# Attention values computed as transposed pairs of heads, with the probabilities normalised before they are transposed

## The chip, the cores and the metric

The kernel runs on one core of a Trainium2 chip. The metric is device microseconds of one execution. The kernel before was timed in three runs: the median is 1093.15 us, from 1092.9 to 1095.22 us.

## The reference

A model of three layers works on one sequence of S = 256 tokens with 1024 channels, in float32. Layer 0 mixes eight "fox" heads and eight "dsa" heads of width 64 (dsa: each query keeps only its 64 best keys, chosen by an index score). Layer 1 has sixteen "moba" heads of width 64; at this length they are causal. Both are followed by a gated feed-forward part with a short convolution. Layer 2 ("second block") mixes eight latent-attention heads ("mla", width 64, mask by chunks of 64) and four mLSTM heads ("ml", width 128), and is followed by a mixture of 32 experts and a gated per-layer embedding. All 36 softmax or mLSTM heads end in the same way, here for softmax:

```python
s = where(mask, (q @ k.T) * scale, -1e30)      # 256 queries x 256 keys, per head
pr = softmax(s, axis=-1)
out[:, h*64:(h+1)*64] = pr @ v                 # per head
x = x + concatenate(all heads) @ w_out         # 1024 x 1024
```

## The kernel before

The program is written by hand for each engine: `tensor` (TensorE, PE), `vector` (VectorE, DVE), `scalar` (ScalarE, ACT), `gpsimd` (POOL) and `sync` (the DMA queue). Every engine executes its own list strictly in order, and semaphores join them. `claim` and `take` give out one of the eight PSUM banks and wait until its last user was drained; `filled` and `emptied` wait for a bank to be complete or drained. Weights (1 MB units) stream into a ring of seven slots (twelve in the expert stage). Each weight chunk is split into a high part (`wh`, ACT, `split_hi`) and a low part (`wl`, DVE, `split_lo`), three chunks deep; activations are split likewise (`hh`/`hl`, `mh`/`ml`), and a product is the three terms high x high, high x low and low x high in the fast float32r format. `out_steps` (L667) computes the output projection of a layer in 16 steps: eight slices k of 128 input channels, each for two tiles t of 128 queries, six matmuls of 512 columns per step.

The attention part of each layer is a software pipeline written out by hand, of 21 iterations i in layers 0 and 1 and of 15 in layer 2. In iteration i PE computes the scores of head h = i (`score_T`, L710), transposes the probabilities of head i-2 (`probs_T`, L700: three 128 x 128 transposes, since query tile 0 sees only key tile 0) and computes the values of head i-3 (`value_T`, L717). Between these it runs steps of the projections of the same layer (`proj`, or `z_pieces` in layer 2), of `side` work (the dsa index and mask in layer 0) and of `out_steps`. Iterations 8 and 9 have no new head in layers 0 and 1: there the second group of eight heads is prepared (in layer 0, POOL rotates the dsa queries, L2625, and PE transposes them into `dqT`). DVE adds the mask and takes row maxima (`maxima`, L1948), ACT takes the exponential and row sums (`probs`, L1363), and the transposed probabilities are copied to `ptb` by ACT or, for even heads of layer 1, by DVE (`evac_P`).

In `value_T` the transposed probabilities (128 keys x 128 queries) are the stationary operand and the 64 value columns of the head move: three matmuls per head, which all write 64 columns of two banks, one for each query tile. After the eighth head of a group DVE divides both banks by the row sums into `mix` (`finish`, L1958), PE transposes `mix` (`mixT`, L840: eight transposes per group, in iteration 10 or 11 for the first group and after the loop for the second; once in layer 2), and ACT and DVE split the result into `mh` and `ml` (`mix_hi` L1372, `mix_lo` L1967). Only then can the slices of that group enter `out_steps`.

In layer 2 the mLSTM heads have a longer way: DVE's `hm_steps` (L2374) normalise the outputs of the four heads (its last step signals `s_hm`), PE transposes them (`hmT`), and DVE and ACT apply the gate and split them; slices k = 4 to 7 of the output projection wait for that. `z_pieces` (L1088) are eight pieces of a projection, handed out in the iterations `z_steps` (L505).

## Time and profile before

| | |
|---|---|
| median of 3 runs | 1093.15 us |
| the profiled execution | 1093.0 us |
| its span, first to last instruction | 1090.9 us |
| PE busy | 1040.6 us (95%) |
| DVE busy, ACT busy | 621.6 us (57%), 521.4 us (48%) |
| granted TensorE clock, mean | 0.983 of 2.4 GHz |
| chain that ended last | PE 89%, DVE 6%, ACT 2% |

The numbers of a stretch or a line come from views of the trace: the timeline lists instructions in order of time, adjacent ones of one kind merged, with the start, the busy time and, in brackets, how long the engine stood idle before it and what released it. A float32 matmul leaves two records (each passes over its columns), a float32r matmul or a transpose one. Records overlap, so the price of a group is the distance from its start to the start of what follows. A form such as 128*64 128x512 means a stationary operand of 128 rows and 64 columns and a moving one of 128 rows and 512 columns.

### The profile page before, as it was taken

What the parts mean: (1) busy time and instruction counts of PE and PEld (TensorE: products, weight loads), DVE (VectorE), ACT (ScalarE), POOL (GpSimd) and SP (SyncE); (2) the same over time, 40 slices, a digit from 0 to 9 for tenths busy, and PEclk for the clock granted to TensorE, in tenths of its full rate; (3) what the DMA queues carried; (4) which work ended last, traced back from release to release, by engine and by line L of the source; (5) the groups of instructions that cost most, each with busy time, mean ns of one, the idle gap of its engine ahead of it and who ended that gap; (6) DMA issues with size and microseconds to landing.
All of it is one profiled execution on the core that took longest, in us unless ns stands there. A gap on an engine that the chain in (4) does not pass through costs nothing.

```text
span 1090.9 us, 15541 instructions
## 1 busy us (share of the span) xinstructions
PE 1040.6 (95%) x6143; PEld 816.4 (75%) x6143; DVE 621.6 (57%) x1167; ACT 521.4 (48%) x902; POOL 90.2 (8%) x104
## 2 busy tenths in 40 slices
PE   6998999999999999899999999989899999999977
PEld 5777789999888877799999888778754545445435
DVE  4677467888746556468888647646662221122146
ACT  5755555555535454456556435755442212122145
POOL 0101001121100311001212101100000000000000
PEclk9999899999999999999999999998989999999999
DMA  8824136655554633245565564207629999999931
GB/s 282 292 78 154 40 116 186 201 157 195 190 192 155 220 117 105 74 145 190 170 201 170 194 180 137 94 30 244 234 75 393 409 408 407 409 409 409 406 127 39
DMA packets 112672, 224.63 MB, mean 206 GB/s; under 512 B 10559, under 2 KB 65234, under 8 KB 112594
## 3 DMA queue, kind: packets, MB, share of 16 engines
q1 hardware_dynamic: 112434, 223.04, 58.1%
q8 instruction: 51, 0.84, 0.3%
q10 hardware_dynamic: 160, 0.53, 0.1%
q14 instruction: 27, 0.22, 0.1%
HBM read 222.50 MB, written 1.05 MB: 205 GB/s over the span
## 4 chain that ended last, share of the span: by engine, by line
PE 89%; DVE 6%; ACT 2%; DMA 1%; issue 1%; POOL 0%; SPq 0%; DVEq 0%; POOLq 0%; ACTq 0%
PE ps L527 84%; PE ps L531 5%; DVE wl L1825 1%; DMA ring<-in_w_uv_dram 1%; ACT hh L1310 1%; DMA cst<-in_const_dram 0%; DVE hl L1835 0%; DVE ml L1825 0%; ACT wh L1313 0%; DVE xs L1825 0%; DVE smb L1839 0%; POOL sA L2625 0%; DVE sA L1835 0%; ACT L1310 0%; ACT sA L1310 0%
## 5 line engine op out<-in xcount | busy, mean ns | idle before, releaser
L1825 DVE TENSOR_TENSOR wl<-ring,wh 128x1024 fp32r<-128x1024 f32 (+3 forms) x212 | 278.2, 1322 | 124.9 <-ACT wh L1313 123.3
L1313 ACT ACTIVATE wh<-ring 128x1024 fp32r<-128x1024 f32 (+3 forms) x212 | 222.5, 1053 | 150.3 <-PE ps L527 148.2
L527 PE MATMUL ps<-hh,wh 128*128 128x256 f32 x768 | 219.5, 287 | 1.3 <-DVE big L1830 1.2
L527 PE MATMUL ps<-hh,wl 128*128 128x256 f32 x768 | 217.2, 284 | 0.0
L527 PE MATMUL ps<-hl,wh 128*128 128x256 f32 x768 | 215.5, 284 | 0.0
L527 PEld LDWEIGHTS ps<-hh,wh 128*128 128x128 f32 x768 | 147.9, 193 | 2.4 <-DVE big L1830 1.5
L527 PEld LDWEIGHTS ps<-hh,wl 128*128 128x128 f32 x768 | 147.9, 193 | 0.0
L527 PEld LDWEIGHTS ps<-hl,wh 128*128 128x128 f32 x768 | 146.9, 193 | 0.3
L527 PE MATMUL ps<-ring,xg 128*64 128x512 f32 x320 | 85.5, 595 | 0.0
L527 PE MATMUL ps<-wh,hh 128*128 128x512 f32 (+3 forms) x192 | 80.1, 417 | 5.3 <-DVE wl L1825 5.1
L2654 POOL TENSOR_TENSOR fs<-fs,rt 128x256 f32<-128x256 f32 x44 | 52.5, 1212 | 324.3 <-ACT fs L1310 324.3
L527 PE MATMUL ps<-wl,hh 128*128 128x512 f32 (+3 forms) x192 | 75.2, 391 | 0.0
L527 PE MATMUL ps<-wh,hl 128*128 128x512 f32 (+3 forms) x192 | 73.6, 391 | 0.0
L1835 DVE SCALAR_TENSOR_TENSOR ysl<-ps,wsl,ysh 128x512 fp32r<-128x512 f32 x32 | 24.0, 751 | 83.0 <-ACT ysh L1310 83.0
L1835 DVE SCALAR_TENSOR_TENSOR fa<-ps,rsl,fs 128x256 f32<-128x256 f32 x16 | 7.7, 484 | 105.7 <-ACT fs L1310 105.7
L527 PEld LDWEIGHTS ps<-ring,xg 128*64 128x64 f32 x320 | 26.4, 137 | 50.4 <-issue 50.3
L527 PE MATMUL ps<-ringx,xg 128*64 128x512 f32 x192 | 57.6, 592 | 0.0
L1310 ACT ACTIVATE fs<-ps,rsl 128x256 f32<-128x256 f32 x16 | 7.6, 476 | 101.4 <-PE ps L527 101.4
L527 PE MATMUL ps<-wl,ffh 128*128 128x512 f32 x176 | 54.9, 389 | 0.0
L527 PE MATMUL ps<-wh,ffl 128*128 128x512 f32 x176 | 54.9, 389 | 0.0
L527 PE MATMUL ps<-wh,ffh 128*128 128x512 f32 x176 | 54.8, 389 | 0.0
L1839 DVE CUSTOM_DVE_ANT_0 smb<-ps,cst 128x128 f32<-128x128 f32 x72 | 25.7, 357 | 44.3 <-PE ps L527 42.7
(273 smaller groups left out, 1719.9 us busy)
## 6 DMA issues: line engine op xcount, KB each, us to landing
ring<-in_w_up_dram SPq DMA_DIRECT2D x88, 512.0 KB, 4.9
ring<-in_w_down_dram SPq DMA_DIRECT2D x22, 1024.0 KB, 4.9
ring<-in_w_gate_e_dram SPq DMA_DIRECT2D x40, 512.0 KB, 7.9
ring<-in_w_up_e_dram SPq DMA_DIRECT2D x40, 512.0 KB, 11.1
ringx<-in_w_down_e_dram SPq DMA_DIRECT2D x16, 1024.0 KB, 10.1
ring<-in_w_down_e_dram SPq DMA_DIRECT2D x16, 1024.0 KB, 11.3
ring<-in_w_in_odd_dram SPq DMA_DIRECT2D x12, 1024.0 KB, 5.0
ringx<-in_w_gate_e_dram SPq DMA_DIRECT2D x24, 512.0 KB, 9.8
```

What stands on the lines that cost most here:

```text
L527: return e.matmul(o, l, r, start=start, stop=stop)
L531: return e.transpose(o, i, cst[0:n, C_ID:C_ID + n])
L1310: return e.activation(o, i, f, **kw)
L1313: return e.activation(o, i, ACT.Copy)
L1825: return e.tensor_tensor(o, a, b, op)
L1835: return e.scalar_tensor_tensor(out=o, in0=a, scalar=s, in1=b, op0=o1, op1=o2)
L1839: return e.tensor_tensor_reduce(out=o, in0=a, in1=b, scale=1.0, scalar=init, op0=o1, op1=o2, accum_out=ac)
L2654: e.tensor_tensor(fs[:, f % 2, :], fs[:, f % 2, :], rb, ALU.mult).then_inc(s_silr, 1)
```

## The change

`value_pair` takes the place of `value_T` for all heads of width 64 (the mLSTM heads keep `value_T`). The values of a head (128 keys x 64 columns) are now the stationary operand and the transposed probabilities move: one matmul of 256 queries for key tile 0 and one of 128 queries for key tile 1. The result is already transposed (64 channels x 256 queries). An even head writes partitions 0 to 63 of the bank and the odd head after it partitions 64 to 127, so that a bank holds four heads, which are two slices k of the output projection. The pair is computed in the iteration of its odd head.

Since queries now lie along the free axis, the division by the row sums moves ahead of the transposes. DVE inverts the sums of each head (`inverted`), and the probabilities are multiplied in place, in two instructions: by ACT for the fox heads and the even moba heads, by DVE for the dsa, the odd moba and the mla heads (`normed`). `probs_T` waits for `s_pn` in place of `s_p`. `finish`, `mixT` and the copy by which DVE made one of the high parts are gone; ACT makes all of them (`mix_hi`) and DVE subtracts (`mix_lo`), one bank at a time, in iterations 8, 10 and 17 and after the loop (layer 0), 11 or 12, 17 and after (layer 1), 10 and after (layer 2).

The output projection runs as one generator over all eight slices: ten, eight and four steps of it are handed out in or right after the loops of layers 0, 1 and 2 (before: seven, seven, none). The z pieces of layer 2 end in iteration 11 and not after the loop, and the mLSTM normalisation has one more of its steps inside the loop. The first four slices of layer 2 have split buffers of their own, and one ring slot of the expert stage is loaded only after slice 3.

```diff
-        out_at = ((12, 13, 14, 15, 16, 18, 19), (13, 14, 15, 16, 17, 18, 19))
-        z_steps = (0, 2, 4, 6, 8, 10, 12, 14)
+        out_at = (range(11, 21), range(13, 21), range(12, 15))
+        z_steps = (0, 2, 4, 6, 8, 9, 10, 11)
...
                 if g in SP:
-                    q.wait_ge(s_p, SP[g])
+                    q.wait_ge(s_pn, SP[g])
...
+            def value_pair(name, bt, vals, ptb):
+
+                def f(h):
+                    n, j = h // 4, h // 2 % 2
+                    gs = [G[name][h - 1], G[name][h]]
+                    b = claim(bt[n], name, n) if j == 0 else bank[bt[n]]
+                    for t in range(2):
+                        for a, g in enumerate(gs):
+                            w = mm(b[64 * a:64 * a + 64, j * S + t * P:(j + 1) * S], vals(h - 1 + a, t),
+                                   ptb[:, g % 3, 2 * t * P:(t + 2) * P], t == 0, t == 1)
...
-            value = [value_T("fox", 8, 64, lambda h, t: big1[:, t, 1024 + h * 64:1088 + h * 64], (0, 1), ptb1),
-                     value_T("dsa", 8, 64, lambda h, t: dv[:, t, h * 64:h * 64 + 64], (6, 7), ptb1)]
-
-            def mixT(layer, g, src):
...
+            value = [value_pair("fox", (0, 1), lambda h, t: big1[:, t, 1024 + h * 64:1088 + h * 64], ptb1),
+                     value_pair("dsa", (6, 7), lambda h, t: dv[:, t, h * 64:h * 64 + 64], ptb1)]
...
-            rotation[:] = [4, 5, 6, 7]
-            mixT(2, 0, "mla")
-            for _ in out_steps((2, "out"), c_outm, range(0, 3), 8, mh3, ml3, mixed(2), high=mixed_high(2)):
-                pass
+            next(outp)
+            rotation[:] = [4, 5, 7, 0]
             q.wait_ge(s_hm, 1)
...
+            def normed(g, h, pb, count):
+
+                q.wait_ge(s_rs, count)
+                act(pb[:, g % 3, 0:P], pb[:, g % 3, 0:P], ACT.Copy, scale=rsi[:, 0, h:h + 1])
+                act(pb[:, g % 3, P:384], pb[:, g % 3, P:384], ACT.Copy, scale=rsi[:, 1, h:h + 1]).then_inc(s_pn, 1)
...
+            def inverted(g, h):
+
+                q.wait_ge(s_p, SP[g])
+                return rcp(rsi[:, :, h:h + 1], rs[:, :, h:h + 1])
+
+            def normed(g, h, pb):
+
+                own.inc(inverted(g, h))
+                for c, t in ((slice(0, P), 0), (slice(P, 384), 1)):
+                    w = ts(pb[:, g % 3, c], pb[:, g % 3, c], rsi[:, t, h:h + 1], None, ALU.mult)
+                    if t == 0:
+                        own.inc(w)
+                w.then_inc(s_pn, 1)
+
+            def mix_lo(name, n, hi_, lo_, count):
+
+                b = filled(q, name, n)
+                q.wait_ge(s_mhi, count)
+                tt(lo_, b[:, :], hi_.bitcast(F32), ALU.subtract).then_inc(of(drained, name, n), 1)
...
+                h = head_at.get(i - 1)
+                if h is not None:
+                    if h < 8:
+                        inverted(h, h).then_inc(s_rs, 1)
+                    else:
+                        normed(h, h, pb1)
+                if i in (8, 10, 17):
+                    n = (8, 10, 17).index(i)
+                    filled(q, ("even", 4), 1)
+                    mix_lo(("fox", "dsa")[n // 2], n % 2, bank_of(mh1, n), bank_of(ml1, n), n + 1)
...
+                if i >= 1 and i <= 12 and order2[i - 1][0] == "mla":
+                    normed(32 + i - 1, order2[i - 1][1], pb3)
...
-                if 10 <= i < 13:
+                if 10 <= i < 14:
                     next(hms)
-            q.wait_ge(s_xn, 2)
-            finish("mla", 8, lambda t: mix[:, t, 0:512])
-            gate_rows(3)
-            mix_lo(2, 0, mh3, ml3, 5)
             for _ in hms:
                 pass
-            for k in range(3):
-                split_lo(c_outm + k + 3, wh, wl)
+            mix_lo("mla", 1, mla_hi[:, 1, :], mla_lo[:, 1, :], 10)
+            split_lo(c_outm + 5, wh, wl)
...
+                elif k == NU + 4:
+                    q.wait_ge(s_mlo, 2)
+                    q.wait_ge(*chunk_done[c_outm + 3])
```

## Rows read from the trace of the kernel before

**Rows 1.** The page, part 1: busy time by engine, over the whole span.
```profile
PE 1040.6 (95%) x6143; PEld 816.4 (75%) x6143; DVE 621.6 (57%) x1167; ACT 521.4 (48%) x902; POOL 90.2 (8%) x104
```

**Rows 2.** PE timeline, layer 0: start, busy us, engine, line, operation; one head's values.
```profile
84.14 0.78 PE L527 MATMUL ps<-big,ptb 128*128 128x64 f32 x6
84.75 1.08 PE L527 MATMUL ps<-ring,sA 128*128 128x512 f32 x2
```

**Rows 3.** PE timeline: one float32 matmul on the whole array; then experts, alternating column halves.
```profile
79.51 1.02 PE L527 MATMUL ps<-ring,sA 128*128 128x512 f32 x2
80.36 0.82 PE L527 MATMUL ps<-mb,big 66*128 66x128 f32 x4
...
854.51 3.60 PE L527 MATMUL ps<-ring,xg 128*64 128x512 f32 x16
857.95 3.60 PE L527 MATMUL ps<-ringx,xg 128*64 128x512 f32 x16
861.48 0.50 PE L527 MATMUL ps<-S__12,xh 128*128 128x256 f32 x2
```

**Rows 4.** PE timeline, layer 2: matmuls in one column half only.
```profile
695.55 3.67 PE L527 MATMUL ps<-big,ring 128*64 128x256 f32 x16
699.15 1.98 PE L527 MATMUL ps<-ring,big 128*128 128x512 f32 x4
```

**Rows 5.** PE timeline, layer 0, between the fox and the dsa heads.
```profile
105.14 1.97 PE L531 MATMUL ps<-cst,big 128*128 128x128 f32 x8 [1.49 <-POOL big L2625]
...
109.43 1.97 PE L531 MATMUL ps<-cst,xs 128*128 128x128 f32 x8
...
114.97 0.88 PE L531 MATMUL ps<-cst,pb 128*128 128x128 f32 x3 [1.98 <-DVE mxb L1839]
```

**Rows 6.** PE timeline, layer 0, after its loop.
```profile
140.01 1.25 PE L531 MATMUL ps<-cst,xs 128*128 128x128 f32 x8 [1.14 <-DVE xs L1825]
141.02 0.71 PE L527 MATMUL ps<-wh,mh 128*128 128x512 f32 x2
```

**Rows 7.** PE timeline, layer 1: the seam between its groups, and after its loop.
```profile
438.08 0.52 PE L531 MATMUL ps<-cst,pb 128*128 128x128 f32 x3 [1.80 <-DVE ptb L1843]
...
461.87 0.33 PE L531 MATMUL ps<-cst,xs 128*128 128x128 f32 x1 [1.07 <-DVE xs L1825]
```

**Rows 8.** PE timeline, layer 2, from the last values to the next norm.
```profile
752.76 1.54 PE L527 MATMUL ps<-big,ptb 128*128 128x64 f32 x6 [1.92 <-ACT ptb L1313]
...
756.77 1.91 PE L531 MATMUL ps<-cst,xs 128*128 128x128 f32 x8
...
767.33 0.72 PE L527 MATMUL ps<-wh,mh 128*128 128x512 f32 x2 [2.38 <-DVE wl L1825]
...
785.34 1.91 PE L531 MATMUL ps<-cst,x 128*128 128x128 f32 x16
```

**Rows 9.** DVE timeline: a reciprocal, a scaling of 256 columns, and the mLSTM's last step.
```profile
98.98 0.35 DVE L1830 TENSOR_SCALAR top<-top,st 128x256 f32<-128x256 f32 x1
...
102.68 0.25 DVE L1851 RECIPROCAL rsi<-rs 128x16 f32<-128x16 f32 x1
...
764.92 1.22 DVE L1825 TENSOR_TENSOR xs<-xs,st 128x1024 f32<-128x1024 f32 x1
```

**Rows 10.** DVE timeline, dsa heads: from one head's maxima over a weight split to the next.
```profile
125.77 0.29 DVE L1839 CUSTOM_DVE_ANT_0 smb<-ps,sA 128x128 f32<-128x128 f32 x1 [2.37 <-PE ps L527]
...
126.65 1.22 DVE L1825 TENSOR_TENSOR wl<-ring,wh 128x1024 fp32r<-128x1024 f32 x1
129.10 0.29 DVE L1839 CUSTOM_DVE_ANT_0 smb<-ps,sA 128x128 f32<-128x128 f32 x1 [1.24 <-PE ps L527]
```

**Rows 11.** ACT timeline: a scaling of 256 columns.
```profile
716.90 0.38 ACT L1310 ACTIVATE mb<-ps 128x256 f32<-128x256 f32 x1
```

**Rows 12.** Windows: length, busy us by engine, PE clock, DMA share, GB/s.
```profile
745.00:760.00 15.00, 12.77 (x80) 12.01 (x79) 9.87 (x22) 7.94 (x19) 0.00 (x0) 0.77 0.58 181
...
940.00:980.00 40.00, 40.00 (x210) 19.76 (x210) 9.48 (x17) 9.30 (x21) 0.00 (x0) 1.00 1.03 409
```

More of the change, by code:

```diff
@@ L450, in build, with halves, tiles, bank_of @@
         hsq = smb3[:, :, :].rearrange("p a b -> p (a b)")[:, 0:1024].rearrange("p (t h d) -> p t h d", t=2, d=P)
+        def halves(v):
+            return [v[:, j * S:(j + 1) * S] for j in range(2)]
+        def tiles(v, ks):
+            return [v[:, k, :] for k in ks]
+        def bank_of(v, n):
+            return v[:, 2 * n:2 * n + 2, :].rearrange("p k s -> p (k s)")
         def aT(c, g):
@@ L907, in tensor @@
                     rotation[:] = [4, 5]
-                if i == 10:
-                    rotation[:] = [0, 1]
-                    mixT(0, 0, "fox")
-                    rotation[:] = [4, 5]
-                    outp = out_steps((0, "out"), c_oute, range(4), 8, mh1, ml1, mixed(0), high=mixed_high(0))
             rotation[:] = [4, 5, 6, 7]
-            mixT(0, 1, "dsa")
             for _ in outp:
-                pass
-            for _ in out_steps((0, "out"), c_oute, range(4, 8), 8, mh1, ml1, mixed(0), high=mixed_high(0)):
                 pass
@@ L1483, in scalar @@
             next(proj)
-            outp = iter(())
+            outp = ahead(c_oute, 8)
             for i in range(21):
+                h = head_at.get(i - 1)
+                if h is not None and h < 8:
+                    normed(h, h, pb1, h + 1)
                 h = head_at.get(i - 2)
@@ L1507, in scalar @@
                         evac(flat(dqT[:, 2 * j:2 * j + 2, :]), "dqT", j)
-                if i == 10:
-                    mix_hi(0, 0, mh1)
-                    outp = ahead(c_oute, 4)
-            next(outp)
-            mix_hi(0, 1, mh1)
+                if i in (8, 10, 17):
+                    n = (8, 10, 17).index(i)
+                    mix_hi(("fox", "dsa")[n // 2], n % 2, bank_of(mh1, n))
+            mix_hi("dsa", 1, bank_of(mh1, 3))
             for _ in outp:
                 pass
-            for k in range(4, 8):
-                split_hi(c_oute + k + 3, wh)
             def ffn(l):
@@ L1571, in scalar @@
             next(proj)
-            outp = iter(())
+            outp = ahead(c_outo, 8)
             for i in range(21):
+                h = head_at.get(i - 1)
+                if h is not None and h % 2 == 0:
+                    normed(16 + h, h, pb2, 9 + h // 2)
                 h = head_at.get(i - 2)
@@ L2157, in vector @@
                     next(side, None)
-                if i == 10:
-                    filled(q, ("even", 4), 1)
-                    mix_lo(0, 0, mh1, ml1, 1)
-                    outp = ahead(c_oute, 4)
-            filled(q, "dsa", 1)
-            finish("dsa", 8, lambda t: mix[:, t, 512:1024], 8)
-            next(outp)
-            mix_lo(0, 1, mh1, ml1, 2)
+            mix_lo("dsa", 1, bank_of(mh1, 3), bank_of(ml1, 3), 4)
             for _ in outp:
                 pass
-            for k in range(4, 7):
-                split_lo(c_oute + k + 3, wh, wl)
             add_x((0, "out"))
@@ L2255, in vector @@
                     moba_T(1, i - 8)
-            finish("moba1", 8, lambda t: mix[:, t, 512:1024], 8)
-            next(outp)
-            mix_lo(1, 1, mh2, ml2, 4)
+            mix_lo("moba1", 1, bank_of(mh2, 3), bank_of(ml2, 3), 8)
             for _ in outp:
                 pass
-            for k in range(4, 7):
-                split_lo(c_outo + k + 3, wh, wl)
             add_x((1, "out"))
```

215 lines of the change are left out of this document (108 added, 107 removed).

## The prediction

> **What bounds the kernel now.** I read the page first: PE is busy 1040.6 us of a 1090.9 us span [rows 1], so only 50 us are idle, and a change pays if it takes time off PE's own list or fills its idle stretches. Next the view of PE's waits, which places the idle time, and the timelines of PE, DVE and ACT around the three attention loops. There the waits sit at the seams of the head groups: for POOL's rotation and for DVE's maxima in layer 0 [rows 5], for DVE's copy in layer 1 and DVE's division after the loops [rows 6, 7], for ACT's copy and DVE's weight split in layer 2 [rows 8]. Inside the loops PE has no gaps. The expert stage behind them has none either, but its DMA share is 1.03 at 409 GB/s [rows 12], which is a rival below.
>
> **Part 1, the value matmuls.** Before, one head costs 84.75 - 84.14 = 0.61 us in six records [rows 2], a pair 1.22 us. After, each head has two records of 256 columns and two of 128. A float32 record of 512 columns takes (80.36 - 79.51)/2 = 0.43 us on the whole array; in the expert stage 16 such records that alternate between the column halves take 3.44 us, 0.215 us each [rows 3]. So the halves run at the same time. In one half alone a 256-column record takes 3.60/16 = 0.225 us [rows 4], so its weight load is hidden. A pair is then 2 x 0.225 + 2 x 0.11 = 0.67 us; the run that is followed by whole-array work lasts 3.53 instead of 3.44 us [rows 3], 0.09 us for a switch, taken twice: 0.87 us, a saving of 0.35 us. Bounds: without the overlap 2 x 0.67 + 0.2 = 1.54 us (a loss of 0.32); with no switch cost and perfect overlap 0.64 us (a gain of 0.58). I take 0.87, because the expert rows have the same alternation, type and stationary width. There are 4 fox, 4 dsa, 8 moba and 4 mla pairs.
>
> The Trainium skill speaks against this: TensorE: Matmul & The Clock Gate, section Part 3: Packing small matmuls, says that weight loads overlap running matmuls only if the row group differs, and two column halves share their rows. By that rule the eight loads of a pair would be exposed. The trace does not agree, at least at 512 columns: 0.215 us leaves no room for a load [rows 3].
>
> **Part 2, transposes and division removed.** Eight transposes cost 141.02 - 140.01 = 1.01 us at full clock [rows 6] and up to 1.97 us at the low one [rows 5]; there are five groups. With them go the waits for DVE's division, 1.14 and 1.07 us [rows 6, 7]. What is late next behind the loops: the last bank needs ACT's high part and DVE's low part, about 1.3 us. The generator still has slices of earlier banks to run (k = 5 in layer 0, k = 4 and 5 in layer 1), at least 2.7 us, so nothing of it shows.
>
> **Part 3, work added.** A DVE-normalised head costs a reciprocal (0.25 us) and two scalings (0.35 us, and at most that for 128 columns) [rows 9], 0.9 us with the gaps; an ACT-normalised one about 0.25 + 0.38 [rows 11], 0.65 us, and 0.25 us on DVE. That is 24 heads on DVE (8 dsa, 8 odd moba, 8 mla) and 16 on ACT (8 fox, 8 even moba). In the dsa and second moba loops DVE needs 0.88 us for the maxima, 1.2 us for a split every second iteration and now 0.9 us, 2.4 us in all, against 3.33 us per iteration [rows 10], of which PE saves 0.2. It fits, at no cost. The new wait of `probs_T` comes an iteration after the normalisation, so it normally finds it done.
>
> **Part 4, seam of layer 0.** In iterations 3 to 7 DVE is already nearly full with the mask; five reciprocals and ACT's scalings ahead of `even_evac(4)` delay POOL's rotation. PE's saving on the fox pairs is lost in that wait, and I add 0.75 us: `dqT` transposes at 105.9 and not 105.14 [rows 5]. In return `mixT` (1.97 us) goes and only one `mix_lo` (0.7 us, after its high part) stands between the maxima of heads 8 and 9. The first output step claims bank 1, which that `mix_lo` drains, so PE still waits, but by 118.9 us two output steps are done where one was done at 118.15. One step is 1.4 us. Net gain 0.65 us. Dsa pairs: 4 x 0.35 = 1.4. Behind the loop 1.14 + 1.01 = 2.15. **Layer 0: 4.2 us.**
>
> **Part 5, layer 1.** Moba pairs: 8 x 0.35 = 2.8, with PE full around them. At the seam the 1.80 us wait [rows 7] is for DVE's copy behind `mix_lo`; with `normed` (0.9) and two subtractions (1.3) in place of three instructions (2.0) that copy comes as late as before, and the vanished `mixT` is swallowed by the wait: 0.2. Behind the loop 1.07 + 1.0. **Layer 1: 5.1 us.**
>
> **Part 6, layer 2.** Before, PE ends at 785.34, after waits of 1.92 and 2.38 us, a `mixT` of 1.91 and cold z pieces [rows 8], with a mean clock of 0.77 [rows 12]. I moved the lists of PE, DVE and ACT forward. PE gets to the end of iteration 11 at 750.0 (before, iteration 12 began at 747.3; two z pieces of some 1.6 us each now stand ahead of it, less what the pairs save). There a new wait appears: `normed` of the last head stands behind 2.5 us of mLSTM work on DVE, PE waits about 1.3 us in iteration 13 (and 2.5 if the weight split of iteration 11 counts fully). Four output steps are done by 759.2. DVE's last mLSTM step ends at 761.0 instead of 764.92 + 1.22 = 766.1 [rows 9]. Then `hmT` 0.9, slices 2 and 3 (5.4), a wait of 0.4 for slice 4's split, slices 4 to 7 (10.9): 778.6, a gain of 6.7. PE still idles twice there and the clock will be low in part as before; I take off 1.5. **Layer 2: 5.2 us.**
>
> **Sum.** 4.2 + 5.1 + 5.2 = 14.5 us off the profiled execution of 1093.0 us, which stands at the median (1093.15): 1078.5 us.
>
> **Rivals.** (a) *The halves do not overlap, or the loads of short records are exposed.* A pair costs 1.54 us. For: the expert records are of 512 columns, these of 128 and 256. Against: the rows of part 1 [rows 3, 4]. 16 pairs count (the fox ones are covered): 16 x 0.67 = 10.7 us less gain, 1089 us. Half of it, 1084, if only the loads show.
>
> (b) *The weight stream of the experts sets the end.* The share is 1.03 [rows 12]. Then all that is gained ahead is lost: 1093 us. Against: PE has no wait there, 40.00 of 40 us, and the queue's waits are for PE to free slots, so PE sets the pace.
>
> (c) *Slower: DVE's `normed` stalls every transpose.* If DVE's list per iteration gets longer than PE's, 3.1 us, each of 24 heads puts its 0.9 us on the path: 21.6 us against a gain of 14.5, 1100 us. Its place is the second half of each loop, and it decides once DVE needs over 3.1 us; I count 2.4, so some 0.7 us of unseen waits per head are wanted.
>
> (d) *More than forecast:* the seams close, the clock stays at 2.4 GHz in layer 2 (1.5 us back), and PE gets the fox pairs (1.4), the seams of layers 0 and 1 (2 to 4): 1072 us.
>
> **Chances.** Forecast (1074 to 1083) 0.60; (a) with its half, 0.13; (b) 0.04; (c) 0.07; (d) 0.16. A measurement here can tell about 0.2%, 2.2 us, from no change. Faster: 0.60 + 0.16 + 0.12 = 0.88; same 0.05; slower 0.07. The range takes (d) and the half of (a): 1071 to 1086.
>
> **What would show it.** A pair should start its successor 0.87 us later (part 1); no transposes of `xs` but the eight of the mLSTM (part 2); no PE idle of a microsecond behind the loops of layers 0 and 1 (part 2); the `dqT` transposes of layer 0 at about 105.9 us, later than before in spite of a faster PE (part 4); the next norm of layer 2 about 14.5 us earlier, and every later stage moved by just that (part 6, and against (b)). It would be wrong if `probs_T` rows carry waits for DVE in mid-loop, or if pairs cost over 1.2 us.

## The result and the profile after

The changed kernel takes 1088.24 us (median of 9 runs, 1085.35 to 1090.53); the kernel before, timed beside it, 1095.22 us (median of 9, 1092.62 to 1101.16). The ratio is 0.9919, with a 95% interval from 0.9899 to 0.9939: some 7 to 9 us faster, where 14.5 were forecast. The direction was right, the size about half, and the time lies 2 us above the upper end of the range. (Timed once more below, the change gave 10.4 us by the medians.)

The profiled execution of the changed kernel took 1089.69 us with a span of 1087.9 us. That is only 3.0 us less than the span before, because the profiled execution of the kernel before is among its fastest (1093.0 us) and this one is slower than its median: the two profiles show where time went, and the medians how much. Page, part 1 (answers to [rows 1]):

```profile
PE 1034.5 (95%) x6023; PEld 795.9 (73%) x6023; DVE 628.7 (58%) x1235; ACT 533.7 (49%) x939; POOL 89.7 (8%) x104
```

PE has 120 records less, DVE and ACT have 68 and 37 more. The mean granted clock was 0.976 of 2.4 GHz, in the execution before 0.983. A first account: span times the missing share of the clock is 1090.9 x 0.017 = 18.5 us before and 1087.9 x 0.024 = 26.1 us after (an upper bound of what the clock cost, since a low clock costs nothing while PE idles). What is left is 1072.4 against 1061.8 us. So by this estimate 10.6 us were gained by work and waits, and up to 7.6 us went to the clock, between these two executions. Not between the kernels as a whole: over the executions timed in the groups below, the median clock of the kernel before was 0.977 or 0.978, that of the changed kernel's 15 executions 0.976. The stages say where the two profiles differ. Each cell is the distance between two starts on PE: from the transposes of the last fox head to the transposes of the next norm (layer 0), and from one norm's transposes to the next (layers 1 and 2, experts).

| us | layer 0, from the seam | layer 1 | layer 2 | experts |
|---|---|---|---|---|
| before | 153.40 - 101.64 = 51.76 | 475.24 - 342.49 = 132.75 | 785.34 - 664.23 = 121.11 | 1057.90 - 785.34 = 272.56 |
| after | 153.06 - 102.47 = 50.59 | 470.72 - 342.14 = 128.58 | 780.55 - 659.72 = 120.83 | 1053.82 - 780.55 = 273.27 |

Layer 1 gave 4.2 us, layer 0 counted from the start only 0.34 (its last fox head came 0.83 us later), layer 2 only 0.28. The experts took 0.7 us more and what follows them 1.1 us more (34.1 against 33.0; 32.9 in the second profile of the changed kernel), which makes up the 3.0 us.

**Layer 0.** PE timeline of the changed kernel from the last fox head on (columns as in [rows 2], to be held against [rows 5]):

```profile
102.47 0.55 PE L546 MATMUL ps<-cst,pb 128*128 128x128 f32 x3 [2.07 <-ACT pb L1326]
103.80 1.05 PE L542 MATMUL ps<-ptb,big 128*64 128x256 f32 x8 [0.78 <-ACT ptb L1329]
104.78 1.97 PE L546 MATMUL ps<-cst,big 128*128 128x128 f32 x8
107.52 1.66 PE L542 MATMUL ps<-sA 64*128 64x128 f32 x8 [0.78 <-ACT sA L1329]
109.11 0.79 PE L542 MATMUL ps<-wh,mh 128*128 128x512 f32 x1
112.61 0.79 PE L542 MATMUL ps<-wh,mh 128*128 128x512 f32 x1 [2.70 <-DVE ml L1853]
...
120.00 1.65 PE L542 MATMUL ps<-sA 64*128 64x128 f32 x4
```

The wait for POOL in [rows 5] is gone, and the query transposes start at 104.78, before 105.14. But the first output step issues one matmul and then stands for 2.70 us at the bank that the second fox evacuation has to drain. DVE and ACT at that moment, from their timelines:

```profile
109.29 0.29 DVE L1867 CUSTOM_DVE_ANT_0 smb<-ps,sA 128x128 f32<-128x128 f32 x1 [4.62 <-PE ps L542]
...
111.86 0.69 DVE L1853 TENSOR_TENSOR ml<-ps,mh 128x512 fp32r<-128x512 f32 x1 [1.60 <-ACT mh L1329]
```

```profile
110.29 0.40 ACT L1326 ACTIVATE pb<-smb,nbb 128x128 f32<-128x128 f32 x1 [2.91 <-DVE nbb L1858]
...
111.19 0.57 ACT L1329 ACTIVATE mh<-ps 128x512 fp32r<-128x512 f32 x1
```

The bank was complete at about 104.8, where the row of its last pair ends. Both engines then idled, DVE for 4.62 us and ACT for 2.91, and turned to the next head's maxima and exponentials first, because those stand ahead of the evacuation in their lists. After this stall the records stay long: windows of 6 us (columns as in [rows 12]) of the kernel after, then before:

```profile
109.00:115.00 6.00, 3.30 (x8) 1.78 (x6) 3.11 (x14) 3.00 (x10) 0.00 (x0) 0.50 0.01 3
115.00:121.00 6.00, 6.00 (x17) 4.20 (x17) 2.74 (x9) 1.76 (x6) 0.00 (x0) 0.50 0.00 0
121.00:127.00 6.00, 6.00 (x22) 3.96 (x21) 2.61 (x15) 2.90 (x8) 0.00 (x0) 0.68 0.00 0
```

```profile
109.00:115.00 6.00, 4.02 (x19) 2.57 (x17) 3.66 (x14) 1.47 (x5) 0.00 (x0) 0.50 0.00 0
115.00:121.00 6.00, 6.00 (x25) 4.57 (x26) 2.66 (x12) 4.57 (x15) 0.00 (x0) 0.76 0.01 3
```

PE is busy for all of 115 to 121 in both, but does 17 records in one and 25 in the other: the clock is at its lower level, 1.2 GHz, to about 124 us instead of 118.

**Layer 1.** PE timeline, then DVE timeline:

```profile
435.36 0.81 PE L546 MATMUL ps<-cst,pb 128*128 128x128 f32 x3 [1.81 <-DVE ptb L1871]
...
455.63 0.55 PE L546 MATMUL ps<-cst,pb 128*128 128x128 f32 x3 [1.53 <-DVE pb L1858]
```

```profile
454.10 0.69 DVE L1853 TENSOR_TENSOR ml<-ps,mh 128x512 fp32r<-128x512 f32 x1 [3.62 <-ACT mh L1329]
```

The first wait is the one of [rows 7], as forecast. The second is new: DVE stood 3.62 us in front of `mix_lo` of iteration 17, for ACT's high part, and the last head's division was queued behind it. The waits behind the loop are gone.

**Layer 2.** PE, DVE and ACT timelines (to be held against [rows 8]):

```profile
718.18 1.08 PE L542 MATMUL ps<-big 2*128 2x128 f32 x4 [1.59 <-DVE rs L1867]
...
750.17 0.90 PE L546 MATMUL ps<-cst,pb 128*128 128x128 f32 x3 [3.29 <-DVE pb L1858]
...
763.24 1.09 PE L546 MATMUL ps<-cst,xs 128*128 128x128 f32 x8 [1.89 <-DVE xs L1853]
```

```profile
746.75 0.69 DVE L1853 TENSOR_TENSOR mla_lo<-ps,mla_hi 128x512 fp32r<-128x512 f32 x1 [3.15 <-ACT mla_hi L1329]
...
748.37 0.29 DVE L1867 CUSTOM_DVE_ANT_0 smb<-ps,cst 128x128 f32<-128x128 f32 x1
...
749.44 0.68 DVE L1858 TENSOR_SCALAR pb<-pb,rsi 128x128 f32<-128x128 f32 x2
```

```profile
745.09 1.05 ACT L1329 ACTIVATE wh<-ring 128x1024 fp32r<-128x1024 f32 x1
746.03 0.58 ACT L1329 ACTIVATE mla_hi<-ps 128x512 fp32r<-128x512 f32 x1
```

The same pattern: `mix_lo` of iteration 10 held DVE for 3.15 us, since ACT makes the high part at the end of its own iteration 10, behind a weight split. The maxima of the last head (head 11 of the 12), whose scores PE had long computed, came only at 748.37, and behind them, at 749.44, the division of head 10. It is head 10 whose transposes PE waits for at 750.17, in iteration 12. In the windows (after, then before) there is also a new stretch at the low clock early in the loop, behind the wait at 718.18:

```profile
715.00:727.00 12.00, 10.41 (x54) 9.05 (x52) 6.65 (x30) 4.14 (x13) 0.00 (x0) 0.72 0.01 2
```

```profile
715.00:727.00 12.00, 11.21 (x73) 9.69 (x72) 5.98 (x28) 6.68 (x20) 0.00 (x0) 0.99 0.00 0
```

### The profile page after: what moved, and what is told of

It reads as the page before. It is cut to its first block, busy times and chain, and to the rows that moved or that the text cites. A ratio compares the mean times of both kernels' runs of the same rounds, so it can differ in the third digit from the quotient of the medians.

```text
span 1087.9 us, 15372 instructions
## 1 busy us (share of the span) xinstructions
PE 1034.5 (95%) x6023; PEld 795.9 (73%) x6023; DVE 628.7 (58%) x1235; ACT 533.7 (49%) x939; POOL 89.7 (8%) x104
## 4 chain that ended last, share of the span: by engine, by line
PE 86%; DVE 7%; ACT 4%; DMA 1%; issue 1%; SPq 0%; DVEq 0%; ACTq 0%
PE ps L542 81%; PE ps L546 4%; DVE wl L1853 1%; ACT pb L1326 1%; DMA ring<-in_w_uv_dram 1%; DVE smb L1867 1%; ACT hh L1326 1%; ACT wh L1329 0%; DMA cst<-in_const_dram 0%; DVE hl L1863 0%; DVE xs L1853 0%; DVE smb L1853 0%; ACT xh L1329 0%; ACT L1326 0%; ACT xg L1326 0%
## 5 line engine op out<-in xcount | busy, mean ns | idle before, releaser
L1326 ACT ACTIVATE ysh<-ps,wsl 128x512 fp32r<-128x512 f32 x32 | 22.0, 687 | 58.9 <-PE ps L542 58.9
```

What stands on the lines that cost most here:

```text
L1326: return e.activation(o, i, f, **kw)
```

## The experiments

**The theory** (W, later Q, for queue): the change's own savings are there, and half of them is lost to DVE and ACT evacuations that stand in the wrong place of two in-order lists, and to the low clock that follows the stalls. Its rivals: the clock's chance in one execution (C), the work on column halves keeping the clock low (V), DVE's or ACT's work itself as the bound (D, A), and the division as the whole cause.

The runs were timed in three groups, each on another chip with the kernel before beside it. Its median was 1098.26 us in the first group (the changed kernel once more, the early fox bank, the mLSTM steps, both heads in one half), 1097.88 in the second (the first latent bank, no division, the four moves, all eight latent heads on ACT) and 1095.87 in the third (steps one iteration later, the four moves again, six latent heads on ACT). The changed kernel was in the first group only. For the other two, a difference from it is therefore given by way of the kernel before: the lead over the kernel before beside it, less the 10.4 us that the changed kernel had.

### The changed kernel once more

> The changed kernel once more, unchanged, as the yardstick of the runs beside it. Theory W (the new waits are a property of the order of work): the same idle stretches as in its first profile stand at the same places, 2.70 us at 112.61 behind the evacuation of the fox bank, 1.59 us at 718.18, 3.29 us at 750.17, and the stretches at the lower TensorE clock follow them (to about 124 us in layer 0). Rival C (the small gain is the clock's chance of one execution): the waits stay, but the low stretch of layer 0 ends near 118 us as in the kernel before, layer 0 ends 2 us or more earlier than 153.1, and the time comes out near 1083.

Measured: 1087.9 us (median of 6, 1085.51 to 1091.14), ratio to before 0.9899 (0.9858 to 0.9941), 10.4 us by the medians. The waits stand where they stood: 2.70 us for `ml`, 1.58 for `rs`, 3.29 and 1.51 for `pb`, and layer 0 takes 51.36 us from the seam, with the clock low to about 125. C falls for layer 0. One wait is new, 0.98 us for the last head's division in iteration 13 of layer 2.

### The second fox bank evacuated early

First ACT in iteration 9, then DVE at the head of iteration 10:

```diff
+                    mix_hi("fox", 1, bank_of(mh1, 1))
                     for j in range(2):
                         evac(flat(dqT[:, 2 * j:2 * j + 2, :]), "dqT", j)
-                if i in (8, 10, 17):
+                if i in (8, 17):
...
+                    filled(q, ("even", 4), 1)
+                    mix_lo("fox", 1, bank_of(mh1, 1), bank_of(ml1, 1), 2)
                     for _ in side:
                         pass
```

> The changed kernel with one thing moved: the evacuation of the second fox bank (ACT's high part, DVE's low part) goes ahead of the dsa queries' evacuation on ACT and to the head of iteration 10 on DVE, where both engines idle (2.3 and 4.6 us), instead of behind the eighth head's maxima and exponentials. Theory W: the 2.70 us wait of the first output step on bank 1 is gone, TensorE is busy through 109 to 113 us, its clock rises near 118 us as before instead of 124, and layer 0 ends about 3.5 us earlier (149.5 instead of 153.1): time 3 to 4.5 us below the changed kernel. Rival V (work on column halves keeps the clock low): the wait goes, but the low stretch still ends at 122 us or later, and the gain is under 2 us.

Measured: 1083.86 us (1079.82 to 1085.24), 4.0 us below, ratio 0.9859 (0.9817 to 0.9900); the two intervals overlap, but the slowest of these runs is faster than the fastest of the changed kernel beside it. The wait is gone. Windows:

```profile
109.00:115.00 6.00, 4.61 (x26) 2.97 (x26) 3.31 (x17) 3.55 (x11) 0.00 (x0) 0.94 0.01 3
115.00:121.00 6.00, 6.00 (x31) 4.17 (x30) 4.61 (x20) 4.50 (x13) 0.00 (x0) 1.00 0.00 0
```

31 records in 115 to 121 instead of 17. From the seam layer 0 took 147.32 - 105.06 = 42.26 us, 8.3 less than in the first profile of the changed kernel. Four later profiles with the early bank give 42.18 to 42.77 us; four with the changed kernel's own layer 0, the first among them, 48.63 to 51.36. The profile gives twice what the median does: this execution reached its seam 2.6 us later, and its layer 1 took 1.5 us more than the same code did before. The time is as expected, the clock is not: it was full from about 110.6, before the first output step, and not from 118. V falls: the pairs on column halves are the same here and the clock is full.

### The output steps begun one iteration later

```diff
-        out_at = (range(11, 21), range(13, 21), range(12, 15))
+        out_at = (range(12, 21), range(13, 21), range(12, 15))
```

> The changed kernel with the output projection's steps of layer 0 begun in iteration 12 instead of 11 (on all engines), and nothing else moved: the wait on the second fox bank, which the first step claims, must vanish by name, but no work takes its place in iteration 11. Theory F (what the early evacuation gained was work for TensorE in the seam, and through it the clock): TensorE idles through most of 109 to 113 all the same, now behind ACT's and DVE's work on the first dsa heads, the clock is low to 118 us at least, and one step more stands after the loop: within 2 us of the changed kernel. Rival N (it is the wait itself that costs): 2.5 us or more below the changed kernel, as with the early evacuation.

Measured: 1084.0 us (1082.68 to 1086.26), ratio 0.9882 (0.9847 to 0.9917), 11.9 us below the kernel before: 1.5 us more than the changed kernel's lead, and the intervals of the two ratios overlap almost whole. (The bare medians differ by 3.9 us, but the kernel before was 2.4 us faster in this group too.) I had expected under 2. PE timeline:

```profile
110.45 0.92 PE L542 MATMUL ps<-sA 64*128 64x128 f32 x4 [0.93 <-DVE mxb L1867]
114.61 0.90 PE L546 MATMUL ps<-cst,pb 128*128 128x128 f32 x3 [3.23 <-DVE pb L1858]
```

```profile
109.00:115.00 6.00, 1.84 (x12) 1.04 (x10) 3.52 (x17) 2.45 (x9) 0.00 (x0) 0.73 0.00 0
115.00:121.00 6.00, 6.00 (x23) 4.11 (x21) 2.76 (x15) 3.59 (x10) 0.00 (x0) 0.71 0.01 3
```

PE idles as I said, even more (1.84 of 6 us busy). But the stalled step had held back what stood behind it in PE's list: the scores of head 10 start at 110.45 here and at 115.04 in the changed kernel, so DVE and ACT go on meanwhile. From the seam layer 0 takes 150.64 - 102.80 = 47.84 us. By these single profiles, 2.8 of the 8.3 us that the early evacuation won from the seam come from not letting PE stand in front of that bank, and the other 5.6 need the bank drained early, so that PE has work in the seam. The clock was full at 108.60 here too (0.93 us for the eight score records, 1.66 in the changed kernel), but behind the wait of 3.23 us it was low again, to about 118. So in these profiles the clock rose at that point with either order, and stayed up only where PE had work. The time is what theory F expected; N, which wanted 2.5 us or more, is not borne out.

### The mLSTM steps moved back

```diff
-                if 10 <= i < 14:
+                if 11 <= i < 15:
                     next(hms)
```

> The changed kernel with the mLSTM epilogue's steps on DVE begun one iteration later in layer 2, so that the last head's division stands ahead of the large step instead of behind it. Theory W: the 3.29 us wait at 750.17 falls under 0.7 us, the low clock of 748 to 757 us goes for the most part (2 us), while the epilogue ends up to 2.5 us later and the wait of the epilogue's transposes (1.89 us at 763.24) grows by about as much: layer 2 ends 1 to 3 us earlier. Rival D (the chain of DVE's work sets the end of layer 2): the wait reappears whole at the epilogue's transposes, and layer 2 ends within 0.7 us of 780.55.

Measured: 1091.06 us (median of 12, 1088.55 to 1096.37), 3.2 us above the changed kernel by the medians, ratio 0.9935 (0.9907 to 0.9963), which overlaps the changed kernel's; the profiled execution, 1095.81 us, is one of the five slower ones of the twelve. Layer 2 took 784.33 - 660.05 = 124.28 us, against 120.83 and 122.08 in the two profiles of the changed kernel. PE timeline:

```profile
749.45 0.84 PE L546 MATMUL ps<-cst,pb 128*128 128x128 f32 x3 [2.27 <-DVE pb L1858]
...
764.39 1.97 PE L546 MATMUL ps<-cst,xs 128*128 128x128 f32 x8 [5.01 <-DVE xs L1853]
```

The wait at head 10 fell by 1.0 us, and the wait for the epilogue grew by 3.1. Only the small first mLSTM step (747.36 to 748.2 in the changed kernel's DVE rows) stood between `mix_lo` and this division, and delaying the steps gave no gain. So theory W, too, had the wrong holder for this wait; the DVE rows of layer 2 above name the right one, `mix_lo`. The large step, which the prediction had named, stands ahead of head 11's division and is not at issue at 750.17.

### The first latent bank evacuated one iteration later by DVE

```diff
-                if i == 10:
+                if i == 11:
                     q.wait_ge(s_xn, 2)
                     mix_lo("mla", 0, mla_hi[:, 0, :], mla_lo[:, 0, :], 9)
```

> The changed kernel with DVE's evacuation of the first latent bank moved from iteration 10 to iteration 11 of layer 2, behind that iteration's maxima and division, so that DVE no longer stands 3.15 us before it for ACT's high part (746.75 in the changed kernel's trace) with the next head's maxima queued behind. Theory Q (the 3.29 us wait of TensorE at 750.17 is DVE's queue behind that evacuation, not the mLSTM's steps as the prediction had it): the wait falls under 1 us, the low clock of 748 to 757 us goes, the epilogue's chain starts some 3 us earlier too, and layer 2 ends 3 to 5 us earlier (117 us or less from nm2's transposes to nf2's, instead of 120.8): 3 to 4.5 us below the changed kernel. Rival D (DVE's own work in iterations 10 to 14 is what TensorE waits for): most of the wait comes back one iteration later and the gain is under 1 us.

Measured: 1086.59 us (1084.21 to 1088.99), ratio 0.9889 (0.9856 to 0.9922): a lead of 11.3 us over the kernel before, about 1 us more than the changed kernel's, less than expected, and not told from it by the intervals. In the trace layer 2 took 776.54 - 661.83 = 114.71 us, 6.1 less than in the first profile (four profiles with the old order here gave 117.5 to 122.1), and its clock was 1.00 in both stretches where it had been low, 718 to 730 and 747 to 759:

```profile
747.95 0.50 PE L542 MATMUL ps<-wh,mla_hi 128*128 128x512 f32 x1 [1.29 <-DVE mla_lo L1853]
751.45 0.55 PE L546 MATMUL ps<-cst,pb 128*128 128x128 f32 x3 [1.25 <-DVE pb L1858]
759.27 1.09 PE L546 MATMUL ps<-cst,xs 128*128 128x128 f32 x8 [2.10 <-DVE xs L1853]
```

The wait of 3.29 us for head 10 is gone: the theory names the right instruction. In its place an output step waits 1.29 us for the moved `mla_lo`, and head 11 waits 1.25 us in iteration 13, the wait that the prediction had forecast (1.3 us); so the rival is right that DVE's work comes due soon after (DVE is busy 11.21 us of 12 in 747 to 759). The waits together fell by only 0.7 us; by this one profile, most of the rest is the clock.

### The division left out

```diff
-                own.inc(inverted(g, h))
-                for c, t in ((slice(0, P), 0), (slice(P, 384), 1)):
-                    w = ts(pb[:, g % 3, c], pb[:, g % 3, c], rsi[:, t, h:h + 1], None, ALU.mult)
...
-                w.then_inc(s_pn, 1)
+                inverted(g, h).then_inc(s_pn, 1)
```

(and `normed` on ACT with its calls; the reciprocal of each head now releases its transposes)

> The changed kernel without the division itself: the reciprocals stay and release the transposes, the 16 divisions on ACT (0.80 us each) and the 24 on DVE (0.67 us each) are left out, so that the probabilities go undivided into the value products. It prices what part 3 of the prediction set at nothing. If part 3 holds, the time stays within 1.5 us of the changed kernel. Theory Q expects 3 to 6 us less: 0.8 us off each of the waits on pb at 99.05, 102.47, 140.68, 455.63 and 750.17 and off the bank wait at 718.18, and what the clock gives back with them; the waits behind the mix evacuations (2.70 at 112.61, most of 3.29 at 750.17) stay. If the division were the whole cause of the missing half, it would be 8 us or more.

This kernel leaves the division by the row sums out, so its values are not the model's. Measured: 1080.36 us (median of 4, 1077.08 to 1083.99), ratio 0.9845 (0.9802 to 0.9888): a lead of 17.5 us over the kernel before, 7.1 more than the changed kernel's (5.9 by the ratios). The remaining waits of the transposes are now on the reciprocal:

```profile
101.61 0.55 PE L546 MATMUL ps<-cst,pb 128*128 128x128 f32 x3 [1.96 <-DVE rsi L1875]
...
739.41 0.55 PE L546 MATMUL ps<-cst,pb 128*128 128x128 f32 x3 [2.58 <-DVE rsi L1875]
```

Every layer is shorter, 46.34, 126.07 and 116.63 us, and the waits at 99.05, 140.68 and 455.63 are gone. So the division costs some 6 to 7 us with this order of work, at or above the upper end of what I expected, and not far from the 8 us that would have made it the whole cause. But it isn't: the next run keeps every division and gains more, 2.7 us in the same group.

### Four evacuations moved, nothing removed

Four moves in DVE's list, of six banks in all: the early fox bank (shown above, on ACT too), the first dsa and the first moba1 bank, moba0's two banks, and the first latent bank. In layer 1 the copy `evac_P` now comes ahead of the block of moba0:

```diff
-                if i in (8, 10, 17):
-                    n = (8, 10, 17).index(i)
+                if i in (8, 18):
+                    n = (8, 10, 18).index(i)
...
+                if i == 18:
+                    mix_lo("moba1", 0, bank_of(mh2, 2), bank_of(ml2, 2), 7)
+                h = head_at.get(i - 2)
+                if h is not None and h % 2 == 0:
+                    evac_P(16 + h, ptb2)
                 if i == 12:
                     filled(q, ("odd", 5), 1)
                     for n in range(2):
                         mix_lo("moba0", n, bank_of(mh2, n), bank_of(ml2, n), 5 + n)
-                if i == 17:
-                    mix_lo("moba1", 0, bank_of(mh2, 2), bank_of(ml2, 2), 7)
-                h = head_at.get(i - 2)
-                if h is not None and h % 2 == 0:
-                    evac_P(16 + h, ptb2)
...
-                if i == 10:
+                if i == 11:
                     q.wait_ge(s_xn, 2)
```

> The changed kernel with four evacuations of DVE put elsewhere in its queue, nothing added or taken away: the second fox bank early (as in the run before it), the first dsa and moba1 banks one iteration later (18 instead of 17), moba0's two behind the copy of the transposed probabilities in iteration 12, the first latent bank in iteration 11. Theory Q: the waits at 112.61 (2.70), 435.36 (1.81), 455.63 (1.53), 140.68 (0.5) and 750.17 (3.29) go or fall under 0.7, and with them most of the low clock in 434 to 440 and 748 to 757: 8 to 12 us below the changed kernel, near 1077, which is what the prediction gave for the change. Rival D: the gains don't add up since DVE's work comes due again, and it ends within 2 us of the seam's edit alone (4 us below the changed kernel).

> The kernel with the four moved evacuations once more, as the yardstick beside the next run: 10 us below the changed kernel, 18 to 21 below the kernel before.

Measured: 1077.61 us (1072.32 to 1078.30), ratio 0.9801 (0.9767 to 0.9836), and again 1074.77 us (1071.97 to 1076.97), ratio 0.9796 (0.9760 to 0.9831). That is 20.3 and 21.1 us below the kernel before beside it, with all of the change's work in it, and 9.9 and 10.7 us more than the changed kernel's lead, as expected of theory Q. The waits of PE that are left in layers 1 and 2 (timeline):

```profile
425.64 0.87 PE L546 MATMUL ps<-cst,pb 128*128 128x128 f32 x3 [0.62 <-DVE ptb L1872]
...
735.84 0.50 PE L542 MATMUL ps<-wh,mla_hi 128*128 128x512 f32 x1 [1.29 <-DVE mla_lo L1854]
739.34 0.55 PE L546 MATMUL ps<-cst,pb 128*128 128x128 f32 x3 [1.27 <-DVE pb L1859]
747.16 1.09 PE L546 MATMUL ps<-cst,xs 128*128 128x128 f32 x8 [2.10 <-DVE xs L1854]
```

and the seam of layer 0 (windows):

```profile
109.00:115.00 6.00, 6.00 (x24) 4.12 (x23) 4.92 (x22) 4.29 (x14) 0.00 (x0) 0.83 0.01 3
115.00:121.00 6.00, 6.00 (x34) 4.18 (x34) 4.59 (x18) 3.90 (x11) 0.00 (x0) 1.00 0.00 0
```

The stages take 42.18, 125.75 and 116.11 us (42.18, 125.78 and 116.16 the second time); the mean clock is 0.988 and 0.987. Over all executions its median is 0.984 and 0.986, against 0.976 in the changed kernel: by the same upper bound as above, 9 to 11 us, so the removed waits and the clock behind them can't be told apart in this gain. Nor does this run show that the moves need the change: the kernel before, whose clock is low in the seam of layer 0 too, was not reordered.

### The latent heads divided by ACT

On top of the four moves, first ACT's list of layer 2, then DVE's; a second version does so for the first six heads only:

```diff
+                if 1 <= i <= 12 and order2[i - 1][0] == "mla":
+                    normed(32 + i - 1, order2[i - 1][1], pb3, 17 + order2[i - 1][1])
...
-                    normed(32 + i - 1, order2[i - 1][1], pb3)
+                    inverted(32 + i - 1, order2[i - 1][1]).then_inc(s_rs, 1)
```

> The four moved evacuations, and in layer 2 the eight latent heads' divisions on ACT (1.60 of its 3 us busy at most in a slice) in place of DVE. Theory Q: the bank wait at 718.18 (1.59 us, DVE's reciprocal, division and weight split ahead of the evacuation) falls to about 0.8, its low clock of 718 to 727 goes (3 us), at no cost on ACT: 1 to 4 us below the run with the four moves alone. Rival A (ACT turns late instead): a wait on ACT's pb of 1 us or more stands in iterations 3 to 12, and it is no faster than the four moves alone.

> The four moved evacuations, and in layer 2 the first six latent heads' divisions on ACT, the last two on DVE, since with all eight on ACT the last one waited 2.60 us on ACT for DVE's reciprocal and held up ACT's weight split and through it DVE's epilogue chain (4.00 us wait at 748.00). Theory Q: the bank wait at 708 keeps its 0.86 us instead of 1.58, the last two heads wait as in the run with the four moves (1.3 us each), the epilogue's transposes wait 2.1 to 2.8 us, and the time is 1 to 2.5 us below the four moves alone. Rival D (the end of layer 2 is DVE's epilogue chain whatever comes ahead of it): within 1 us of the four moves alone.

Measured: 1075.46 us (1074.32 to 1077.88), ratio 0.9794 (0.9761 to 0.9826), with all eight on ACT, 2.2 us below the four moves in the same group; 1076.63 us (1073.48 to 1078.52), ratio 0.9803 (0.9766 to 0.9839), with six, 1.9 us above the four moves in its group, where theory Q wanted 1 to 2.5 below. Neither can be told from the four moves alone. The bank wait fell to 0.86 us as expected, and with all eight on ACT the price came back at the epilogue (PE, then DVE timeline):

```profile
748.00 1.97 PE L546 MATMUL ps<-cst,xs 128*128 128x128 f32 x8 [4.00 <-DVE xs L1856]
```

```profile
741.04 1.23 DVE L1856 TENSOR_TENSOR wl<-ring,wh 128x1024 fp32r<-128x1024 f32 x1 [2.47 <-ACT wh L1329]
```

DVE, freed of the divisions, waits 2.47 us for a weight split that ACT reaches late; layer 2 took 119.46 us in this profile, against 116.11 with the four moves alone. Six on ACT avoids that (2.10 us at the epilogue) and still gains nothing measurable. That fits rival D for the end of layer 2.

### Both heads of a pair in one half

```diff
-                    for t in range(2):
-                        for a, g in enumerate(gs):
-                            w = mm(b[64 * a:64 * a + 64, j * S + t * P:(j + 1) * S], vals(h - 1 + a, t),
+                    for a, g in enumerate(gs):
+                        for t in range(2):
+                            w = mm(b[0:64, j * S + t * P:(j + 1) * S], vals(h - 1 + a, t),
```

> The changed kernel with the second head of every pair written to the same partition half of the bank as the first, one head after the other (the second head's values overwrite the first's, and the upper half of the bank is not computed): same matmuls, same columns, no two of them in different halves. Part 1 of the prediction says that the halves run at once: a pair of 8 records then costs 1.3 us (768 columns at the 0.43 us per 512 of two passes each way) instead of 0.80, and 20 pairs cost up to 10 us, some of it hidden in the waits of layer 2 and of the seam: time 6 to 10 us above the changed kernel. The rival of part 1 (halves don't run at once, the loads set the pace): the pair stays at 0.8 to 0.9 us and the time moves by under 2 us.

This kernel leaves out the upper half of each bank and overwrites one head's values with the other's. Measured: 1096.55 us (median of 10, 1095.27 to 1100.68), 8.7 us above the changed kernel in the same group; ratio to before 0.9996 (0.9967 to 1.0024). The groups of fox, moba and latent values, by form, of the changed kernel and of this one (busy us in total, mean ns):

```profile
L542 PE MATMUL ps<-ptb,big 128*64 128x256 f32 x64 | 10.9, 420 | 0.8 <-ACT ptb L1329 0.8
L542 PE MATMUL ps<-ptb,big 128*64 128x128 f32 x64 | 6.7, 288 | 0.0
```

```profile
L542 PE MATMUL ps<-ptb,big 128*64 128x256 f32 x64 | 20.3, 399 | 0.8 <-ACT ptb L1329 0.8
L542 PE MATMUL ps<-ptb,big 128*64 128x128 f32 x64 | 12.6, 279 | 0.0
```

17.6 us become 32.9 for 16 pairs. A merged pair row goes from 0.87 to 1.51 us; from its start to the start of what follows, where nothing waits, a pair goes from 0.80 to 1.45 us (127.64 to 128.44 in the changed kernel, 133.04 to 134.49 here). 20 pairs at 0.65 us would be 13 us; 8.7 show in the time. With nothing but the side-by-side placement gone, the kernel is as slow as the one before.

## Why the prediction was half right

**Part 1 (the pair) held.** 0.87 us were forecast from one start to the next (its own terms, 0.67 + 2 x 0.09, add up to 0.85). Measured that way a pair costs 0.80 us, so it saves 0.42 us and not 0.35; that the merged row also reads 0.87 is chance, since such a row overlaps its successor. In one half a pair costs 1.45 us, where the prediction had 1.54 for no overlap. The bound of rival (a) is about right and the rival itself is refuted by the run in one half. The change covers 20 pairs, 40 of the kernel's 44 heads (not 36, as the section on the reference has it). The Trainium skill (TensorE: Matmul & The Clock Gate, Part 3: Packing small matmuls) says that weight loads overlap running matmuls only if the row group differs. This case's rows don't agree, for records of 128 and 256 columns either: the eight loads of the pair at 127.64 take 136 ns each in the mean of their group, 1.1 us if they stood one after the other, and the whole pair is over in 0.80 us.

**Part 2 held.** No transposes of `mix` but the mLSTM's are left, and PE goes through the ends of the loops of layers 0 and 1 without a wait.

**Part 3 (the added work fits at no cost) failed.** It compared sums: 2.4 us of DVE's work against 3.33 of PE's, less 0.2. A head cost about what I said, 0.16 + 0.67 us on DVE and 0.80 on ACT where I had 0.65. Yet without the divisions the kernel is 6 to 7 us faster, and `probs_T` rows do wait for DVE inside the loops (0.52, 1.53 and 3.29 us), which the prediction had named as a sign of being wrong. What counts is where a division stands: between a head's exponentials and its transposes, behind whatever blocks DVE's list. The list was blocked at four places, at each of which DVE waited for ACT's high part (1.60, 3.62 and 3.15 us), or subtracted two banks ahead of the copy to `ptb` (1.81 us on PE; this one the prediction had).

**Part 4 (seam of layer 0): 4.2 us forecast, 0.34 measured.** The queries' transposes came at 104.78, not 105.9, so that term erred to the safe side. The step that failed is the one on the first output step: "PE still waits, but by 118.9 us two output steps are done". They were done at 120.0, and the clock was priced at nothing, though [rows 5] showed it low there already: to about 124 us each step and each head cost nearly double. Of the 3.9 us that are missing, about 1.1 had gone by 120.0; the 4.9 us to 124.9 would be some 2.5 us shorter at the full clock (an estimate, at half the time each), and 0.5 is the wait at 140.68. The early evacuation, which removes the wait on the bank, shortens layer 0 from the seam by 8.3 us in the trace and the kernel by 4.0 in the medians.

**Part 5 (layer 1): 5.1 forecast, 4.2 measured.** The mechanism was right, but the total is closer than its halves. Up to the seam's transposes (95.59 us into the layer before, 93.22 after) 2.4 us were gained where the pairs and the seam should give 1.6; from there to the end 1.8 where 3.5 were forecast, and the missing 1.7 is about the wait of 1.53 us at 455.63 that I had not seen. With that wait and most of the 1.81 us removed the layer takes 125.75 us, 2.8 less.

**Part 6 (layer 2): 5.2 forecast, 0.28 measured.** The forecast's times are those of the kernel before, whose layer 2 begins at 664.23; the changed kernel's begins at 659.72, so both are counted from there. The step that failed is "DVE's last mLSTM step ends at 761.0", 96.8 us into the layer. It ended at 761.96 + 1.23 = 763.2, 103.5 us into the layer: 6.7 us late, and 1.6 later than before. What follows it took 17.3 us, where the forecast has 17.6, so this one term holds the whole miss. Two waits ahead of it were not in the forecast: 3.29 us in iteration 12, behind `mix_lo`, and 1.59 us in the fourth iteration (before, 0.79 in its place), with the low clock behind each (0.72 in 715 to 727, where the kernel before had 0.99). The wait that was forecast, 1.3 us in iteration 13 behind the mLSTM's step, is another one, and it was right: hidden in the first profile by the delays ahead of it, 0.98 us in the second, 1.25 us once `mix_lo` was moved. With that one move DVE's step ends 97.4 us into the layer and the layer takes 114.71 us; with all four moves it takes 116.1. The forecast was 115.9.

**The rivals.** (c) put the price on every transpose, 24 times 0.9 us; the truth is a few transposes with 1 to 3 us each. (b) is not it: the experts took 273.27 instead of 272.56 us, so 0.7 us of the lead was lost there, no more, and that small loss was not traced further; with a lead of 20 us it was 1.0 (273.57). The extra wait of one ring slot's load was not tried by itself. (d), 21 us below the kernel before, is about where the four moves led (20 and 21), by causes named there (seams closed, clock up), but only after an edit that the forecast kernel did not have.

What stays open is the split of the missing 4 to 7 us: the waits, the divisions and the clock are not additive. The removal of the divisions gives 6 to 7 us, the four moves 10 to 11, the single moves 4.0 and about 1.

## What to carry to other kernels

When work is added to an in-order engine, don't ask whether it fits the iteration's sum; ask which waiting instruction stands ahead of it, and put an evacuation that needs another engine's half one iteration behind that half, or early where both engines idle. Price a stall of PE by what stands behind it in PE's own list and by the slow records that follow, not by its own length. Before giving up a change that gives half its worth, move the waits: here the same work, reordered at four places, gave 20 to 21 us instead of 7 to 10. And when a forecast for one stage is held against a trace, count both from the start of that stage.

## What the runs showed of the hardware

The lower clock outlives its cause. In layer 0 of the changed kernel PE had no gap from 113 us on, and it was still granted 1.2 GHz to about 124; with the four moves, and 6.00 us busy in 109 to 115, it was back at 2.4 GHz by about 112.

A stall can bring it on anew. In the run with only the latent bank moved, whose layer 0 is that of the changed kernel, the clock was full before the wait on the fox bank and low behind it; the transposes that end the low stretch are in the last row (PE timeline):

```profile
110.47 0.93 PE L542 MATMUL ps<-sA 64*128 64x128 f32 x8 [0.78 <-ACT sA L1329]
...
114.83 0.80 PE L542 MATMUL ps<-wh,mh 128*128 128x512 f32 x1 [2.99 <-DVE ml L1853]
...
123.53 0.55 PE L546 MATMUL ps<-cst,pb 128*128 128x128 f32 x3
```

Whether a given gap brings it on differs between executions. The wait of 1.58 us in the fourth iteration of layer 2 was the same in nine profiled kernels with the same order of work there, and PE was busy 10.4 of 12 us around it each time; the mean clock of these 12 us was 0.72 three times, 0.86 twice and 1.00 four times. Two of them, the changed kernel once more and the four moves once more:

```profile
717.00:729.00 12.00, 10.42 (x51) 8.74 (x50) 6.22 (x32) 4.66 (x14) 0.00 (x0) 0.72 0.01 2
```

```profile
705.00:717.00 12.00, 10.42 (x75) 8.64 (x74) 9.12 (x42) 6.14 (x17) 0.00 (x0) 1.00 0.01 2
```

51 records against 75 in the same time. The Trainium skill (TensorE: Matmul & The Clock Gate, Part 1: The HAM clock gate) says of a kernel's start that the count of slow matmuls varies from run to run; these rows show the same in mid-kernel. So one profile can misstate a stage by 2 to 3 us in either direction, and the executions of the changed kernel spread over 6 us, those of the kernel before over 15. Layer 2 alone, unchanged in the compared code, took 117.5 to 122.1 us.
